# Twenty pairs ahead of the spread of gates in place of thirty, thirty-six within it in place of twenty-two

## The reference

```python
q = (xt @ w_pq).reshape(n_tok, 8, 2, 64)
s1, s2 = q[:, :, 0] @ sub_keys1.T, q[:, :, 1] @ sub_keys2.T      # 128 keys each
v1, i1 = top_k(s1, 16); v2, i2 = top_k(s2, 16)
sc, ic = top_k(v1[..., :, None] + v2[..., None, :], 16)          # over the 256 sums
experts = i1[ic // 16] * 128 + i2[ic % 16]                       # 16 of 16384, per head
gate = softmax(sc)
act = gelu(sum(u_tab[experts] * x, -1))                          # rows of 1024
y = sum(gate * act * v_tab[experts], experts)                    # rows of 1024
out = layer_norm(ALPHA * h + y)
```

## Time and profile before

| | us |
|---|---|
| median of 3 runs (1773.19 to 1776.67) | 1775.95 |
| the profiled execution | 1776.89 |
| its span | 1775.1 |
| TensorE busy | 1671.6 (94%) |
| DVE busy | 1191.9 (67%) |
| POOL busy | 639.4 (36%) |
| ACT busy | 233.9 (13%) |
| DMA moved | 510.53 MB, mean 288 GB/s |

### The profile page before, as it was taken

The page is one execution under the profiler, slowest core; times in us unless marked ns, Lnnn a source line. Parts: engine busy times, 40 slices in busy tenths (PEclk is TensorE's granted clock), DMA queues, the critical chain, the costliest instruction groups (busy, mean ns, idle before and its releaser), DMA issues.

```text
span 1775.1 us, 18587 instructions
## 1 busy us (share of the span) xinstructions
PE 1671.6 (94%) x6812; PEld 1161.5 (65%) x6812; DVE 1191.9 (67%) x2475; ACT 233.9 (13%) x487; POOL 639.4 (36%) x536
## 2 busy tenths in 40 slices
PE   7999999989999779999997889999999999999996
PEld 6588878986655466888876556666666666544442
DVE  4253147221478769999976999786876776666666
ACT  1101024101112102211211121101101101000000
POOL 1000000000146723111664444666545546385540
PEclk9999999999999899999998999999999999999998
DMA  7713400674589976566998889999999999999995
GB/s 234 239 47 101 142 30 1 212 249 150 166 272 350 396 261 249 184 204 200 399 409 310 251 253 326 410 409 409 409 410 410 410 410 409 340 408 409 410 409 208
DMA packets 211622, 510.53 MB, mean 288 GB/s; under 512 B 14487, under 2 KB 109720, under 8 KB 210212
## 3 DMA queue, kind: packets, MB, share of 16 engines
q0 software_dynamic: 74672, 271.55, 40.1%
q1 hardware_dynamic: 136860, 237.79, 37.9%
HBM read 497.71 MB, written 16.29 MB: 290 GB/s over the span
## 4 chain that ended last, share of the span: by engine, by line
PE 68%; DVE 19%; DMA 9%; issue 2%; POOL 1%; ACT 0%; SPq 0%; DVEq 0%; ACTq 0%
PE ps L680 67%; DMA arena<-in_v_tab_dram 3%; DMA arena<-in_v_tab_dram,experts 3%; DVE arena L1402 2%; DVE arena L1387 2%; DVE arena L1428 2%; DMA arena<-in_w_o_dram 2%; DVE i L1321 1%; DMA arena<-in_w_mem_kv_dram 1%; PE ps L692 1%; DVE arena L1391 1%; DVE pos L1336 1%; DVE hotg L1391 1%; DVE arena L1468 1%; DVE v L1320 1%
## 5 line engine op out<-in xcount | busy, mean ns | idle before, releaser
L680 PE MATMUL ps<-arena 128*128 128x256 f32 (+5 forms) x5848 | 1502.4, 418 | 50.6 <-DMA arena<-in_w_in_dram 10.1
L680 PEld LDWEIGHTS ps<-arena 128*128 128x128 f32 (+2 forms) x5848 | 1015.9, 188 | 524.4 <-issue 282.4
L642 POOL DMA_INDIRECT arena<-in_u_tab_dram,experts x256 | 335.1, 1309 | 752.8 <-DVE dots L1402 434.8
L1428 DVE SCALAR_TENSOR_TENSOR arena<-arena,coef 128x1024 f32<-128x1024 f32 x232 | 298.7, 1288 | 107.3 <-DMA arena<-in_v_tab_dram,experts 106.7
L1402 DVE CUSTOM_DVE_ANT_0 arena<-arena 128x1024 f32<-128x1024 f32 x256 | 311.9, 1222 | 87.4 <-DMA arena<-in_u_tab_dram,experts 87.1
L654 POOL DMA_INDIRECT arena<-in_v_tab_dram,experts x256 | 293.8, 1148 | 158.2 <-DVE arena L1428 102.6
L949 ACT ACTIVATE arena<-ps 128x256 f32<-128x256 f32 (+2 forms) x212 | 89.2, 427 | 694.6 <-PE ps L680 655.9
L949 ACT ACTIVATE arena<-ps,bT 128x128 f32<-128x128 f32 (+2 forms) x68 | 36.6, 538 | 305.6 <-PE ps L680 305.5
L1285 DVE TENSOR_TENSOR arena<-arena,ps 128x128 f32<-128x128 f32 (+1 forms) x32 | 13.4, 418 | 80.0 <-PE ps L680 67.9
L635 POOL DMA_DIRECT2D arena<-in_ln_g_dram x1 | 0.6, 550 | 142.9 <-PE ps L680 142.9
L680 PE MATMUL ps<-hT_low,w_high 128*128 128x512 f32 x128 | 50.0, 391 | 0.0
(11 more groups left out here) (131 smaller groups left out, 795.0 us busy)
## 6 DMA issues: line engine op xcount, KB each, us to landing
arena<-in_u_cols_dram SPq DMA_DIRECT2D x128, 512.0 KB, 6.8
arena<-in_v_tab_dram SPq DMA_DIRECT2D x128, 512.0 KB, 6.8
arena<-in_w_in_dram SPq DMA_DIRECT2D x37, 1024.0 KB, 5.5
arena<-in_w_o_dram SPq DMA_DIRECT2D x8, 1024.0 KB, 12.7
arena<-in_w_pq_dram SPq DMA_DIRECT2D x8, 1024.0 KB, 5.2
gates_kept<-arena SPq DMA_DIRECT2D x16, 512.0 KB, 5.7
arena<-gates_kept SPq DMA_DIRECT2D x8, 1024.0 KB, 10.4
beta_copies<-beta_rows SPq DMA_DIRECT2D x1, 4608.0 KB
```

Of the source, the lines that this page charges most:

```text
L642: nc.gpsimd.indirect_dma_start(out=u_ring[:, n % ROWS, :], out_offset=None, in_=u_tab[0], in_offset=bass.IndirectOffsetOnAxis(ap=experts[: ...
L680: return nc.tensor.matmul(dst, lhsT, rhs, start=start, stop=stop, skip_group_check=True)
L1428: nc.vector.scalar_tensor_tensor(out=y_acc, in0=row, scalar=by, in1=y_acc, op0=ALU.mult, op1=ALU.add).then_inc(v_used, 1)
```

## The change

It moves pairs between stages; no instruction is added or removed other than that a pair in stage 2 has its `v` row weighed by TensorE (diagonal and matmul) and not by DVE.

```diff
-REST_PAIRS = 30
+REST_PAIRS = 20
 TOP_LATE, TOP_SOON, LATEST = 46, 53, 116
-X_PAIRS = (22, 0)
-V_PAIRS = (100, PAIRS_IN - TAIL_PAIRS - NORM_PAIRS - TOP_PAIRS - REST_PAIRS - sum(X_PAIRS) - 100)
+X_PAIRS = (36, 0)
+V_PAIRS = (98, PAIRS_IN - TAIL_PAIRS - NORM_PAIRS - TOP_PAIRS - REST_PAIRS - sum(X_PAIRS) - 98)
```

## The result

The changed kernel takes 1787.41 us (median of 5 runs, 1784.31 to 1795.38) against 1773.49 for the kernel before in the same session: ratio 1.0075, 95% interval 1.0059 to 1.0091. That is 13.3 us more by the ratio (10.5 to 16.1); the forecast was +14.5. The profiled execution took 1784.31, its span 1782.5, 7.4 more than before. It reached the normalisation of tiles 1 to 3 (line 1130) 3.6 us earlier than before (651.45 against 655.07), in code that is the same in both; so I compare stretches, not clock times. In a row of a timeline stand the start in us, the duration, engine and line; in brackets how long the engine stood idle before it, and what released it.

What follows compares the result with a forecast made beforehand. TensorE was taken to bind the table dots and V0 and pace V1, DVE the spread, with hand-over waits between. -12.5 + 16.5 + 10.8 - 0.3 = +14.5 us gave 1790.4 us, eight in ten between 1782 and 1798.

Steps and rivals of the forecast that it cites:

- step 1: Ahead of the spread: ten rest pairs leave, TensorE's waits and half clock before ET go; -12.5 us, bounds -9.9 to -13.
- Step 2: In the spread: 13 more dots and a second coefficient, +1 us for transfers; +16.5 us in all.
- second rival: Transfers bind the spread, 147 us against 137: +10 in place of +1, 1800 us; chance 0.12.
- Step 3: Hand-over from spread to V0: a top and one more row delay the start of table_sums(0), +10.8 us, bounds +1.8 to +12.
- first rival: The end of the spread hides the top: hand-over +1.8 to +5, time 1782 to 1785 us; chance 0.09.
- Step 4: V0 and V1 with two pairs fewer each: V0 0 us, V1 -0.3 us from fewer waits.
- third rival: V1 gives back all the freed transfer time, -5.1 us: 1785.6 us; chance 0.07.
- fourth: Transfers, not TensorE, pace the table stages: rest pairs -26, V0 and V1 -10.3, net -10, 1766 us; chance 0.05.

Runs made afterwards that it cites:

- top8_early: The changed kernel with the top behind pair 116 moved to behind pair 81, the last rest pair: ratio 1.0049 to the kernel before.
- before_top_handover: The kernel before with only one top moved, from behind pair 116 to behind pair 113, no pair changing stage: ratio 1.0057, +10.1 us.
- late_exps: The changed kernel with ACT's exponentials of the top behind pair 116 put behind the last diagonal: ratio 1.0078 to the kernel before.
- x24_v65: The kernel before with 24 pairs in the spread and 65 in place of 67 in V1, 30 rest pairs kept: ratio 1.0003.

## Why the prediction was right

It was right in direction and mechanism. In size it was right in the sum, with the gain of step 1 put too high; by its steps:

- **Step 1** (-12.5 us). The wait ahead of ET and the half clock behind it went, as said, and DVE stood 23.8 us for the 20 forecast. The size was taken from a single execution. Its 9.94 us were 4.3 and 4.2 in two others with 30 pairs: in the three, `shares` ends 109.3 to 111.1 us behind line 1363, while the gelu of block 60 starts 101.2 to 106.7 us behind it. The stretch fell by 13.5 us in the profiled pair, but by 9.9 in the mean of all profiled executions, the smaller of the bounds given. The runs say less still. If the other stretches are taken off each kernel's time, an estimate, the eight other kernels with fewer rest pairs leave 6.5 to 8.8 us for this one, mean 7.9, each with an interval of 1.6 to 4.0 us either way; the changed kernel leaves 12.4. Where I wrote three or four pairs, two do.
- **Step 2** (+15.5 and +1 for the transfers). 133.6 us against 118.2, +15.4: 13 dots of 1.15 us and the second coefficient. The +1 was nothing: takes stayed 4.21 us apart, so the second rival falls. Its 3.3 us for a pair's packets were 3.1 in the changed kernel (74.2% of 133 us for 33.81 MB), and with the stored gates' 20.1% the engines' share was 0.94, where it is 1.02 in V0.
- **Step 3** (+10.8). Measured 13.8 - 3.1 = 10.7 us. Its parts show one by one: 9.0 go with the top, 1.7 stay for the second row, and TensorE restarts at half clock. Two small errors cancel: the first row started 7.8 us behind the last take and not 8.3, and the half clock cost 2.3 us and not 1.8. The first rival falls.
- **Step 4** (-0.3 in V1, 0 in V0). V1 is on average 229.8 us with 65 pairs (five executions) and 230.3 with 67 (five), -0.4 within a scatter of 3. The third rival (-5.1) falls. The fourth, that transfers pace the table stages, wanted -26 us from the ten rest pairs and -10.3 from V0 and V1: the former gave 10 at most, eight of the pairs nothing, and V0 and V1 did not move.

Summed with the means of the stretches the change should cost -9.9 + 15.4 + 10.7 - 0.4 = +15.8 us; the runs gave +13.3 (10.5 to 16.1). With the 7.9 us that the other kernels' runs leave for step 1 it would be +17.8, above that interval. So that the forecast of +14.5 lay so near is in part luck: step 1 was put 2.6 to 4.6 us too high, step 2 by 1 us, and the five runs of the changed kernel came out faster than the other kernels let expect. Why is open, as is what moves the start of line 1130 by 4.9 us (651.45 to 656.30) from run to run.

## What to carry to other kernels

Work moved into a stage also moves what is hung on its items: here a top came along with pair 116 and cost 9.0 us by the stretch (4.6 by the runs of top8_early, 10.1 by those of before_top_handover), because it fell into a place where ACT's and TensorE's written order let nothing pass it. When an engine waits at a hand-over, count how much earlier its releaser has to be and move just that; two pairs brought the whole gain, eight more brought nothing there and cost 1.15 us each in the spread. Before pricing a wait from one trace, ask which side of it is steady: only the steady side tells what removing it gives.

## What the runs showed of the hardware beyond what was expected

In late_exps TensorE came back at half clock from a wait of 3.6 us: the block of dots behind it took 5.2 us in place of 3.46, 1.7 more. What the half clock cost did not grow with the wait (ahead of ET by the rows of TensorE and ACT, in the hand-over by the spacing of the weight loads):

| wait of TensorE, us | kernel | lost at half clock, us |
|---|---|---|
| 3.6 | late_exps | 1.7 |
| 4.2 | x24_v65, ahead of ET | 2.6 |
| 4.3 | before_top_handover, ahead of ET | 1.8 |
| 6.8 | before_top_handover, hand-over | 1.6 |
| 6.8 | after, hand-over | 2.3 |
| 9.9 | before, ahead of ET | 2.4 |

Ahead of ET the transposes are part of it: the four took 1.33 us before and in x24_v65, against 0.66 in the changed kernel, and block 61 then took 5.3 and 5.6 us up to its gelu in place of 3.6. So the prediction's 1.8 us in step 1 left out 0.7 us. Of two waits, the short one is the dearer for its size.
